# Attention steps placed between projection and gate passes of a conditioned hybrid decoder layer

## The chip, the cores and the metric

The kernel runs on one core of a Trainium2 chip. A core has a matrix engine (TensorE, PE in the profile, PEld for its weight loads), VectorE (DVE), ScalarE (ACT), GpSimd (POOL) and SyncE (SP), whose queue issues all DMA transfers here. Each engine runs its own instructions in program order; between engines only semaphores order the work. The metric is the device time of one execution in microseconds, the median of several runs.

## The reference, cut to what matters

One decoder layer for two request groups with shared weights: a prompt of 512 tokens and 8 samples of 4 new tokens each, 544 token columns in all, width 1024.

```python
def decoder_layer(x, c, lw, rel_bias, past):
    mod = (jax.nn.silu(c) @ lw['w_ada'] + lw['b_ada']).reshape(B, N_SUB, 3, D_MODEL)
    h = x + 0.5 * mod[:, 0, 2][:, None] * swiglu(modulate(x, gn[0], ...), lw['w_ffn1_gu'], lw['w_ffn1_down'])
    mix, state = token_mixer(modulate(h, gn[1], ...), lw, rel_bias, past)
    h = h + mod[:, 1, 2][:, None] * mix
    h = h + 0.5 * mod[:, 2, 2][:, None] * swiglu(modulate(h, gn[2], ...), lw['w_ffn2_gu'], lw['w_ffn2_down'])

def token_mixer(u, lw, rel_bias, past):
    q, kv_c, kv_s, kv_w, g_nsa, h_cv, b_cv, c_cv, g_merge = split_projection(u, lw['w_in'])
    o_nsa = ...   # compressed + selected + window attention, each branch with its own gate
    y_cv, conv_new = short_conv(h_cv, b_cv, c_cv, lw['w_conv'], conv_buf)
    merged = g_merge[:, :, 0] * (o_nsa @ lw['w_nsa_out']) + g_merge[:, :, 1] * (y_cv @ lw['w_conv_out'])
    return merged @ lw['w_out'], (kv_c, kv_s, win_new, conv_new)
```

`split_projection` applies a sigmoid to the 24 attention gates `g_nsa` and to the 2 x 1024 merge gates `g_merge`. The prompt has 8 blocks of 64 keys, so a selection of 16 takes them all; a sample has 17 and drops one of them by the compressed scores, and reads its past keys and values through a page table.

## The kernel before

Activations are held transposed, features on the partitions, 544 token columns in the free direction. Every product is made of three fp32r products: weights and activations are each split into a high half (ScalarE copies it, `split`, `wh`) and a low half (VectorE subtracts, `lo`, `wl`), and TensorE adds high times high, high times low and low times high. The work is cut into numbered *units*: one unit is one 128-column block of a weight matrix, loaded by SP into one of 4 `raw` buffers, split into one of 2 `wh`/`wl` buffers, and used by 48 matmuls of 272 columns (8 tiles of 128 rows), or 24 for matrices of 512 rows. I call the matmuls of one unit a *pass*. A unit's result fills two PSUM banks (`out2(slot)`), from which VectorE or ScalarE takes it.

The stages in time order: conditioning and compression of the cached keys; norm 0 and feed-forward 1; norm 1; 23 units of the input projection (`U_WIN`: queries, keys and values, attention gates, then four groups of three for the short convolution); 8 pairs of a merge gate unit and a convolution output unit (`U_MGB`); 8 units of the other merge gates (`U_MGA`), with the transposes of the values among them; compression of the prompt's keys (L1522); attention; then the output projection of attention (`U_NSA`), `U_OUT`, norm 2 and feed-forward 2. Nothing plans the order: it is the order in which each engine's code is written.

Attention has 24 prompt *jobs* (query block, branch, half of the heads). In each, TensorE makes four scores (L1603), VectorE adds the bias and takes the maximum (`p_add`, L1231), ScalarE takes the exponential (L815), VectorE scales (`p_scale`, L1251), TensorE transposes (L1615), ScalarE copies (`pTp`, L845), and TensorE multiplies by the values (L1628). The samples are done in two half batches of ten steps each, one step behind each job from the third on (`sample_step`): step 0 scores the new keys, 1 to 3 the cached ones, 4 sums the compressed probabilities and chooses the block that is dropped, 5 scales, 6 and 7 transpose, 8 multiplies by the values, 9 transposes the result.

Between a norm and its first unit VectorE and ScalarE produce the operand tiles one after the other (`u_lo`), and the first unit takes each as it comes (`ready`).

## Time and profile before

| | us |
|---|---|
| median of 3 runs (1538.55 to 1539.65) | 1538.82 |
| the profiled execution | 1537.42 |
| its span, first to last instruction | 1535.6 |
| TensorE busy in it | 1438.0 |
| VectorE, ScalarE, GpSimd busy | 555.3, 464.1, 112.9 |

The profile comes from one execution. [...] A wait is put down to the instruction whose semaphore came last. Instructions overlap by some tenths of a microsecond, so that the distance between two starts says more than a duration. Stages: norm 1 ends with the first matmul of the input projection at 591.05, the merge gates end at 862.50, and the output projection of attention starts at 1025.96.

### The profile page before, as it was taken

To read this page: it belongs to the slowest core of one execution; us is meant where nothing else is said; L and a number is where in the kernel's file an instruction comes from. 1 tells how busy PE (TensorE), PEld (TensorE's weight loads), DVE (VectorE), ACT (ScalarE), POOL (GpSimd) and SP (SyncE) were. 2 spreads that over 40 slices of the span, in tenths; PEclk is the share of its full clock that TensorE was granted. 3 is DMA by queue.
4 is the path that set the end of the run, shared out by engine and by line. 5 is a ranking of instruction groups with operands and counts; after the bars stand their busy time and mean duration, and the time that the engine had idled before them with its cause. 6 is when DMAs were issued, how large, how long until landed. Compare 5 with 4: busy or idle time off the path is not lost.

```text
span 1535.6 us, 28068 instructions
## 1 busy us (share of the span) xinstructions
PE 1438.0 (94%) x11334; PEld 1324.6 (86%) x11334; DVE 555.3 (36%) x1151; ACT 464.1 (30%) x751; POOL 112.9 (7%) x122
## 2 busy tenths in 40 slices
PE   7997999999999996999998989889789999999996
PEld 5676999999999996999998835459789999999995
DVE  0106323332323225335323274745443233232324
ACT  0115333332311114122212346643253333332111
POOL 0402000000001112000000000004320000000110
PEclk9998999999999997999999869989889999999998
DMA  9893444444433232232284323313212322323321
GB/s 347 291 369 110 139 162 137 163 137 161 133 92 87 84 103 54 86 93 69 83 97 157 126 81 102 99 50 116 83 56 82 95 83 86 92 65 87 86 84 67
DMA packets 83541, 180.21 MB, mean 117 GB/s; under 512 B 18341, under 2 KB 43429, under 8 KB 81742
## 3 DMA queue, kind: packets, MB, share of 16 engines
q1 hardware_dynamic: 83470, 179.23, 37.6%
q8 instruction: 49, 0.80, 0.2%
q14 instruction: 22, 0.18, 0.0%
HBM read 173.07 MB, written 10.28 MB: 119 GB/s over the span
## 4 chain that ended last, share of the span: by engine, by line
PE 86%; ACT 4%; DVE 4%; DMA 2%; SPq 2%; issue 2%; ACTq 0%; DVEq 0%
PE PS L1411 71%; PE PS L1334 4%; PE PS L1432 2%; DMA raw<-in_w_in 2%; PE PS L1603 1%; PE PS L1615 1%; SPq L574 1%; DVE rinv L937 1%; PE PS L1438 1%; PE PS L1315 1%; ACT uh L704 1%; PE PS L1348 1%; SPq L562 1%; PE PS L1628 1%; ACT sp L815 1%
## 5 line engine op out<-in xcount | busy, mean ns | idle before, releaser
L1411 PE MATMUL PS<-uh,wh 128*128 128x272 f32 x2032 | 428.8, 292 | 34.9 <-DVE ul L955 26.9
L930 DVE TENSOR_TENSOR wl<-raw,wh 128x1024 fp32r<-128x1024 f32 (+2 forms) x215 | 239.8, 1116 | 587.4 <-ACT wh L679 587.1
L679 ACT ACTIVATE wh<-raw 128x1024 fp32r<-128x1024 f32 (+2 forms) x215 | 203.6, 948 | 816.6 <-PE PS L1411 803.1
L1411 PE MATMUL PS<-uh,wl 128*128 128x272 f32 x2032 | 422.3, 290 | 0.0
L1411 PE MATMUL PS<-ul,wh 128*128 128x272 f32 x2032 | 421.7, 289 | 0.0
L1411 PEld LDWEIGHTS PS<-uh,wh 128*128 128x128 f32 x2032 | 320.5, 190 | 38.9 <-issue 36.1
L1411 PEld LDWEIGHTS PS<-ul,wh 128*128 128x128 f32 x2032 | 321.8, 190 | 0.0
L1411 PEld LDWEIGHTS PS<-uh,wl 128*128 128x128 f32 x2032 | 320.2, 190 | 0.0
L1411 PE MATMUL PS<-hh,wh 128*128 128x272 f32 x704 | 145.7, 288 | 0.9 <-DVE tmp L1004 0.9
L1411 PE MATMUL PS<-hh,wl 128*128 128x272 f32 x704 | 145.7, 288 | 0.0
L1411 PE MATMUL PS<-hl,wh 128*128 128x272 f32 x704 | 145.1, 288 | 0.0
L1411 PEld LDWEIGHTS PS<-hh,wh 128*128 128x128 f32 x704 | 110.7, 188 | 1.1 <-DVE tmp L1004 1.1
L1411 PEld LDWEIGHTS PS<-hl,wh 128*128 128x128 f32 x704 | 110.6, 188 | 0.0
L1411 PEld LDWEIGHTS PS<-hh,wl 128*128 128x128 f32 x704 | 109.9, 189 | 0.0
L1004 DVE TENSOR_TENSOR tmp<-sg,PS 128x544 f32<-128x544 f32 x44 | 31.8, 722 | 181.1 <-PE PS L1411 181.1
L615 POOL TENSOR_TENSOR sq<-h 128x544 f32 x28 | 30.6, 1093 | 857.3 <-DVE h L973 801.9
L1334 PE MATMUL PS<-ch,w 128*128 128x256 f32 x256 | 57.7, 387 | 0.7 <-DVE Fsb L891 0.7
L1334 PEld LDWEIGHTS PS<-ch,w 128*128 128x128 f32 x256 | 49.5, 195 | 8.6 <-issue 1.7
L1615 PEld LDWEIGHTS PS<-cst,sp 128*128 128x128 f32 (+4 forms) x192 | 23.5, 149 | 33.1 <-issue 24.2
L1615 PE MATMUL PS<-cst,sp 128*128 128x128 f32 (+4 forms) x192 | 38.9, 326 | 7.9 <-DVE sp L1251 7.8
L815 ACT ACTIVATE sp<-sp,stp 128x128 f32<-128x128 f32 (+7 forms) x96 | 44.5, 466 | 3.4 <-DVE stp L1235 3.3
L845 ACT ACTIVATE pTp<-PS 128x512 f32<-128x512 f32 (+4 forms) x48 | 28.1, 590 | 44.7 <-PE PS L1615 44.5
(221 smaller groups left out, 1244.5 us busy)
## 6 DMA issues: line engine op xcount, KB each, us to landing
raw<-in_w_gu SPq DMA_DIRECT2D x88, 512.0 KB, 3.6
ada_t<-in_w_ada_t SPq DMA_DIRECT2D x44, 512.0 KB, 4.4
raw<-in_w_in SPq DMA_DIRECT2D x39, 512.0 KB, 3.6
ada<-in_w_ada SPq DMA_DIRECT2D x7, 2048.0 KB, 9.7
raw<-in_w_dn SPq DMA_DIRECT2D x32, 384.0 KB, 3.1
raw<-in_w_dn SPq DMA_DIRECT2D x32, 320.0 KB, 2.9
ch<-in_cmp_pages SPq DMA_DIRECT2D x64, 128.0 KB, 4.1
kv<-in_sel_pages SPq DMA_DIRECT2D x128, 64.0 KB, 1.9
```

The lines of the kernel that those rows point to most:

```text
L562: e.dma_start(kv[:, b, 4 * part + j, :], d["sel_pages"][v][bass.ds(r, 1)].rearrange("o p n -> (o p) n")).then_inc(kv_in[1 + part], 16)
L574: e.dma_start(gs[32 * b:32 * b + 32, hb, br:br + 1], bass.AP(tensor=d["gscr"].tensor, offset=br * NH * TS + SQ * (4 * hb + b), ap=[[TS, NH ...
L615: e.tensor_tensor(sq[:, :], h[:, bass.ds(k, 1), :].rearrange("p o t -> p (o t)"), h[:, bass.ds(k, 1), :].rearrange("p o t -> p (o t)"), AL ...
L679: e.activation(wh[:, u % SPLITS, 0:n, :], raw[:, u % RAWS, 0:n, :], ACT.Copy).then_inc(hi_ready, 1)
L815: e.activation(sp[j % 3][:, r, 0:n], sp[j % 3][:, r, 0:n], ACT.Exp, bias=stp[:, j % 3, 0, r:r + 1], accum_out=stp[:, j % 3, 1, r:r + 1]).t ...
L845: e.activation(pTp[0:n, tr % 2, :], PS[0:n, 4 + tr % 2, :], ACT.Copy).then_inc(p_trc, 1)
L930: e.tensor_tensor(wl[:, u % SPLITS, 0:n, :], raw[:, u % RAWS, 0:n, :], f(wh[:, u % SPLITS, 0:n, :]), ALU.subtract).then_inc(lo_ready, 1)
L1004: e.tensor_tensor(halves(tmp[:, fi % 2, :]), halves(sg[:, fi % 2, :]), out2(2 * (fi % 2) + 1), ALU.mult).then_inc(psum_free, 2)
L1334: ins = mm(PS[:, 2 * (t % 2) + c, 1 - m:257 - m].rearrange("p (g j n) -> p g j n", g=2, n=8), w1[:, c, 8 * m + lp, :], ch[:, t % 2, :, lp, ...
L1411: ins = mm(o[:, a, :], w[:, u % SPLITS, k, :], x[:, k0 + k, HT * a:HT * a + HT], start=(first and k == 0 and w is wh and x is xh), stop=(l ...
L1432: ins = mm(PS[32 * q:32 * q + 32, ada_bank(fi), 0:P], csil[:, k, :], ada_t[:, n % 2, k, :], start=(k < 4), stop=(k >= 4), skip_group_check ...
L1615: ins = e.transpose(PS[0:n, 4 + tr % 2, P * s:P * s + P], sp[j % 3][:, s, P * kt:P * kt + n], ident)
```

## The change

- The 8 convolution output units (`U_CO`) follow the 23 of the input projection directly, and VectorE only copies their result (`mB`). All 16 merge gate units (`U_MG`) come behind them and share one pair of PSUM banks (`GATE_SLOT`).
- The gate units are cut into pieces of one operand tile, 6 matmuls (`fill`). Two whole units stand at the start of the prompt's attention, the other 112 pieces between scores, transposes and value products of the 24 jobs. ScalarE takes each gate out as a tanh of half the input, and splits the next weights behind it (`gate`). The sigmoid is rebuilt as tanh plus one, with the factor one half in `mods`; GpSimd multiplies and adds the convolution half (16 operations).
- The sample steps stand behind projection units (`SAMPLE_AT`): the first half batch behind blocks 10 to 19, the second behind blocks 20 to 22 and the first five convolution output units, its last two steps behind the first two gate units. The unit with the attention gates is moved forward to block 4, the transposes and the compression of the prompt's keys go behind blocks 9 to 14. PSUM slots in the projections are 3 instead of 4, score banks 3 instead of 4.
- SP issues page copies, biases, gate scalars and outputs between the weight loads of those units.
- Behind each norm the first two units run together, tile by tile (`two_units`).
- At the end of the first down projection and of `U_OUT`, VectorE's last `lo` stands behind the last residual.
- The two convolution states are packed by GpSimd into `conv_st` and sent in two transfers.

```diff
+WIN_BLOCK = [0, 1, 2, 3, 10, 4, 5, 6, 7, 8, 9] + list(range(11, 23))
...
+        SAMPLE_AT = {10 + k: (0, k) for k in range(10)}
+        SAMPLE_AT.update({20 + k: (1, k) for k in range(8)})
...
+                elif n == 5:
+                    attention_bias()
+                elif n == 6:
+                    cached_window(0, 0)
+                elif n in (7, 8):
+                    cached_pages(0, 0, n - 7)
...
+                load(U_CO + m, d["w_co"][m])
+                if m == 1:
+                    e.wait_ge(v_used, 1)
+                    cached_window(1, 0)
+                elif m in (2, 3):
+                    cached_pages(1, 0, m - 2)
...
+                elif m == 6:
+                    e.wait_ge(s_work, S_ITEMS + 4)
+                    cached_window(1, 1)
+                elif m == 7:
+                    cached_pages(1, 1, 0)
+            for x in range(2 * KD):
+                load(U_MG + x, d["w_in"][23 + x])
+                if x == 0:
+                    cached_pages(1, 1, 1)
+                elif x == 2:
+                    e.wait_ge(unit_used, U_MG)
+                    for g in range(2):
+                        e.dma_start(toep_g[g][:, :, :], d["toep"][:, GQ * g:GQ * g + GQ, :]).then_inc(toepg_in, 16)
...
                     for m in range(KD):
+                        e.wait_ge(gate_free, m + 1)
+                        e.wait_ge(psum_free, O_CO + m + 1)
+                        e.tensor_tensor(sgB[:, m % 2, :], sgB[:, m % 2, :], mB(m), ALU.mult).then_inc(gated, 1)
+                        e.wait_ge(gated, m + 1)
+                        e.tensor_tensor(mB(m), mB(m), sgB[:, m % 2, :], ALU.add).then_inc(mb_ready, 1)
+                    e.wait_ge(mb_ready, KD)
+                    for m in range(KD):
                         e.wait_ge(psum_free, O_NSA + m + 1)
-                        e.tensor_tensor(work(m), work(m), mB[:, m, :], ALU.add).then_inc(m_ready, 1)
...
+            def gate(x):
+
+                e.wait_ge(unit_used, U_MG + x + 1)
+                if x < KD:
+                    if x >= 2:
+                        e.wait_ge(mb_ready, x - 1)
+                    dst = sgB[:, x % 2, :]
+                else:
+                    dst = sgA[:, x - KD, :]
+                e.activation(halves(dst), out2(GATE_SLOT), ACT.Tanh, scale=0.5).then_inc(gate_free, 1)
+                split(U_MG + x + 2)
...
                 for m in range(KD - 2, KD):
-                    for j in range(4):
+                    for j in range(3 if m == KD - 1 else 4):
                         if ud + 4 * m + j + 2 < U_END:
                             lo(ud + 4 * m + j + 2)
                     e.wait_ge(unit_used, ud + 4 * m + 4)
                     residual(m, 0, gate, m % 2, od, n)
+                if ud + 4 * KD + 1 < U_END:
+                    lo(ud + 4 * KD + 1)
...
+                if n in SAMPLE_AT:
+                    s_step(*SAMPLE_AT[n])
+            for m in range(KD):
+                lo(U_CO + m + 2)
+                e.wait_ge(unit_used, U_CO + m + 1)
+                if m == 0:
+                    e.wait_ge(kv_out, 6 * 16)
+                    e.wait_ge(conv_packed, 2)
+                e.tensor_copy(halves(mB(m)), out2((23 + m) % 3)).then_inc(psum_free, 1)
+                if 23 + m in SAMPLE_AT:
+                    s_step(*SAMPLE_AT[23 + m])
...
             p_add(0)
-            sample_queries()
+            lo(U_MG + 2)
+            s_output(1)
+            lo(U_MG + 3)
...
+                for at_ in fills(j - 1) if j else ():
+                    if (j - 1, at_) in GATE_DONE:
+                        lo(U_MG + GATE_DONE[j - 1, at_] + 2)
             lo(U_NSA + 1)
...
             for m in range(KD):
-                lo(U_OUT + m + 2)
+                if m < KD - 1:
+                    lo(U_OUT + m + 2)
                 e.wait_ge(unit_used, U_OUT + m + 1)
                 residual(m, 0, 24 + 16, m % 4, O_OUT, KD)
+            lo(U_OUT + KD + 1)
...
+            def two_units(u, slot, xh, xl, ready):
+
+                e.wait_ge(lo_ready, u + 2)
+                for k in range(KD):
+                    e.wait_ge(ready[0], ready[1] + k + 1)
+                    for v in range(2):
+                        o = out2(slot + v)
+                        for w, x in ((wh, xh), (wh, xl), (wl, xh)):
+                            for a in range(2):
+                                ins = mm(o[:, a, :], w[:, (u + v) % SPLITS, k, :], x[:, k, HT * a:HT * a + HT],
+                                         start=(k == 0 and w is wh and x is xh), stop=(k == KD - 1 and w is wl))
+                        if k == KD - 1:
+                            ins.then_inc(unit_used, 1)
+
...
+                def first_tile():
+
+                    e.wait_ge(psum_free, og)
+                    two_units(ug, 0, uh, ul, (u_lo, 8 * nn))
+                    if first:
+                        late_partial(0, 0)
+                        e.wait_ge(part_copied, NADA + 1)
+                        late_partial(1, 0)
+                        e.wait_ge(ada_copied, NADA)
+                        late_total(0, 0)
...
-            for n in range(23):
-                if n >= 4:
-                    e.wait_ge(psum_free, O_WIN + n - 3)
-                unit(U_WIN + n, n % 4, uh2, ul2, 0, True, True, 0, (u_lo, 8) if n == 0 else None)
-            for m in range(KD):
-                e.wait_ge(psum_free, O_MGB - 1 + m if m < 2 else O_MGB + 2 * m - 2)
-                unit(U_MGB + 2 * m, 2 * (m % 2), uh2, ul2, 0, True, True)
-                unit(U_MGB + 2 * m + 1, 2 * (m % 2) + 1, yh, yl, 0, True, True, 0, (y_lo, 0) if m == 0 else None)
-
...
+            two_units(U_WIN, 0, uh2, ul2, (u_lo, 8))
+            for n in range(2, 23):
+                if n >= 3:
+                    e.wait_ge(psum_free, O_WIN + n - 2)
+                unit(U_WIN + n, n % 3, uh2, ul2, 0, True, True)
+                if n == 9:
+                    prep_values(0)
+                elif n == 11:
+                    prep_values(1)
+                elif n == 12:
+                    prep_compress()
+                elif n == 13:
+                    prep_keys()
+                elif n == 14:
+                    prep_tails()
+                if n in SAMPLE_AT:
+                    s_step(*SAMPLE_AT[n])
+            for m in range(KD):
...
+            chunk = [0]
+
+            def fill(n):
+
+                for _ in range(n):
+                    x, k = divmod(chunk[0], KD)
+                    chunk[0] += 1
+                    if k == 0:
+                        e.wait_ge(lo_ready, U_MG + x + 1)
+                        if x:
+                            e.wait_ge(gate_free, x)
+                        else:
...
+
+            def p_score(j, s):
                 i, br, _ = JOBS[j]
...
-            p_score(0)
-            p_score(1)
+            e.wait_ge(psum_free, O_CO + KD)
+            for s in range(3):
+                p_score(0, s)
+            fill(KD)
+            s_step(1, 8)
+            p_score(0, 3)
+            for s in range(3):
+                p_score(1, s)
+            fill(KD)
+            s_step(1, 9)
+            p_score(1, 3)
...
-                    p_score(j + 2)
-                if sample_step(j):
-                    s_step(*sample_step(j))
-                for tr in range(TR0[j], TR0[j + 1]):
-                    p_turn(j, tr)
+                more = j + 2 < len(JOBS)
+                if more:
+                    p_score(j + 2, 0)
+                    p_score(j + 2, 1)
+                fill(1)
+                if more:
+                    p_score(j + 2, 2)
+                fill(1)
+                for t in range(turns(j)):
+                    p_turn(j, TR0[j] + t)
+                    if t == 0 and more:
+                        p_score(j + 2, 3)
+                    fill(1)
                     if late:
                         p_value(*late)
-                    late = (j, tr)
+                    late = (j, TR0[j] + t)
+                if "end" in fills(j):
+                    fill(1)
             p_value(*late)
 
 
+            e.wait_ge(gate_free, 2 * KD)
```

Two places in the order of instructions. The first is on ScalarE, at the last convolution blocks of the input projection. Before (`wh` is a split, `yh` the high half of the convolution result):

```order
L679 ACTIVATE wh<-raw 128x1024 x3
L761 ACTIVATE yh<-tmp 128x544
L679 ACTIVATE wh<-raw 128x1024 x2
L679 ACTIVATE wh<-raw 128x512
L761 ACTIVATE yh<-tmp 128x544
L679 ACTIVATE wh<-raw 128x1024
```

After, from the end of block 16's transposes (`pT` are copies of transposed sample probabilities, `sx` is the sample result on its way to the last transpose, `oh` its high half, `ss` a sample exponential):

```order
L825 ACTIVATE pT<-PS 63x128
L744 ACTIVATE wh<-raw 128x1024 x2
L869 ACTIVATE yh<-tmp 128x544
L836 ACTIVATE sx<-PS 128x128
L840 ACTIVATE oh<-PS 64x4x4 x8
L744 ACTIVATE wh<-raw 128x1024
L831 ACTIVATE ss,st<-ss,st 128x63
L744 ACTIVATE wh<-raw 128x512
L831 ACTIVATE ss,st<-ss,st 128x544
```

Sample copies now stand behind `yh`, which itself waits for VectorE's convolution; before, only splits stood there.

The second is on TensorE, in the first job with 512 keys. Before (`kT,qT` scores, `cst,sp` transposes, `pTp` value products, `cst,ss` transposes of the samples):

```order
L1603 MATMUL PS<-kT,qT 128x512 x4
L1615 MATMUL PS<-cst,sp 31x128 x4
L1628 MATMUL PS<-pTp,vcp 64x256 x2
L1603 MATMUL PS<-kT,qT 128x512 x4
L1571 MATMUL PS<-cst,ss 128x128 x8
L1615 MATMUL PS<-cst,sp 128x128 x4
L1628 MATMUL PS<-pTp,vcp 64x256 x2
L1615 MATMUL PS<-cst,sp 128x128 x4
L1628 MATMUL PS<-pTp,vn 64x256 x2
L1615 MATMUL PS<-cst,sp 128x128 x4
```

After (`uh`, `ul` with `wh`, `wl` are the gate pieces of L1746):

```order
L1760 MATMUL PS<-kT,qT 128x512 x2
L1746 MATMUL PS<-uh,wh 128x272 x2
L1746 MATMUL PS<-ul,wh 128x272 x2
L1746 MATMUL PS<-uh,wl 128x272 x2
L1760 MATMUL PS<-kT,qT 128x512
L1746 MATMUL PS<-uh,wh 128x272 x2
L1746 MATMUL PS<-ul,wh 128x272 x2
L1746 MATMUL PS<-uh,wl 128x272 x2
L1772 MATMUL PS<-cst,sp 128x128 x4
L1760 MATMUL PS<-kT,qT 128x512
L1746 MATMUL PS<-uh,wh 128x272 x2
L1746 MATMUL PS<-ul,wh 128x272 x2
```

The four scores of a job are pulled apart, and six gate matmuls stand between each pair of steps.

## Rows read from the trace of the kernel before

**Rows 1.** The page, section 1 and the clock by slice of 38.4 us.

```profile
PE 1438.0 (94%) x11334; PEld 1324.6 (86%) x11334; DVE 555.3 (36%) x1151; ACT 464.1 (30%) x751; POOL 112.9 (7%) x122
...
PEclk9998999999999997999999869989889999999998
```

**Rows 2.** Windows: length, busy time (count) of each engine, clock, DMA share, GB/s.

```profile
598.90:862.50 263.60, 255.87 (x2042) 255.42 (x2043) 89.11 (x126) 56.74 (x70) 0.00 (x0) 0.99 0.38 97
862.50:1025.96 163.46, 138.06 (x974) 76.62 (x972) 98.46 (x479) 89.46 (x291) 0.00 (x0) 0.83 0.31 90
873.00:889.50 16.50, 14.34 (x81) 8.36 (x80) 11.41 (x82) 10.39 (x46) 0.00 (x0) 0.50 0.51 157
812.07:815.49 3.42, 3.42 (x20) 3.42 (x20) 1.26 (x2) 0.00 (x0) 0.00 (x0) 0.64 0.72 188
590.00:600.00 10.00, 8.71 (x44) 8.03 (x45) 8.76 (x13) 8.59 (x14) 7.55 (x13) 0.70 0.00 1
```

**Rows 3.** Timeline of TensorE, attention stage: start, duration, instruction, idle before and releaser.

```profile
907.33 4.39 PE L1603 MATMUL PS<-kT,qT 64*128 64x512 f32 x8 [3.99 <-DVE stp L1231]
...
928.60 1.99 PE L1603 MATMUL PS<-kT,qT 64*128 64x512 f32 x8
```

**Rows 4.** Timeline of ScalarE, projections: two splits that wait for passes.

```profile
606.76 1.06 ACT L679 ACTIVATE wh<-raw 128x1024 fp32r<-128x1024 f32 x1 [4.91 <-PE PS L1411]
...
612.74 1.06 ACT L679 ACTIVATE wh<-raw 128x1024 fp32r<-128x1024 f32 x1 [4.91 <-PE PS L1411]
```

**Rows 5.** Timeline of TensorE, attention stage, single operations.

```profile
862.50 7.25 PE L1522 MATMUL PS<-chp,w1p 128*128 128x64 f32 x64
...
892.16 1.06 PE L1557 MATMUL PS<-kv,qb 128*32 128x512 f32 x8
...
939.04 2.83 PE L1586 MATMUL PS<-kv,pT 128*32 128x128 f32 x96
...
949.38 0.65 PE L1628 MATMUL PS<-pTp,vn 128*64 128x256 f32 x4
...
949.96 0.66 PE L1615 MATMUL PS<-cst,sp 128*128 128x128 f32 x4
```

**Rows 6.** Timeline of TensorE, first pass behind the second norm.

```profile
591.05 0.79 PE L1411 MATMUL PS<-uh,wh 128*128 128x272 f32 x2 [9.02 <-DVE ul L955]
591.64 0.66 PE L1411 MATMUL PS<-ul,wh 128*128 128x272 f32 x2
592.09 0.66 PE L1411 MATMUL PS<-uh,wl 128*128 128x272 f32 x2
```

**Rows 7.** Timeline of VectorE, end of the first down projection.

```profile
576.76 1.23 DVE L930 TENSOR_TENSOR wl<-raw,wh 128x1024 fp32r<-128x1024 f32 x1 [2.53 <-ACT wh L679]
...
577.90 0.50 DVE L965 SCALAR_TENSOR_TENSOR h<-PS,mods,h 128x272 f32<-128x272 f32 x1
...
582.13 0.72 DVE L935 TENSOR_SCALAR rinv<-PS 128x544 f32<-128x544 f32 x1 [3.03 <-PE PS L1424]
```

**Rows 8.** Timeline of ScalarE, a convolution block of the projections.

```profile
678.44 1.06 ACT L679 ACTIVATE wh<-raw 128x1024 fp32r<-128x1024 f32 x1 [4.92 <-PE PS L1411]
...
684.00 0.66 ACT L761 ACTIVATE yh<-tmp 128x544 fp32r<-128x544 f32 x1 [4.50 <-DVE tmp L1094]
```

**Rows 9.** Timeline of VectorE, sample steps 4 and 5.

```profile
902.35 0.22 DVE L1181 COPY sx<-PS 128x63 f32<-128x63 f32 x1 [1.62 <-PE PS L1563]
...
912.95 0.76 DVE L1208 TENSOR_SCALAR ss<-ss,st 128x1056 f32<-128x1056 f32 x1
```

**Rows 10.** Timeline of TensorE, first gate pass after late weights.

```profile
811.71 0.79 PE L1411 MATMUL PS<-uh,wh 128*128 128x272 f32 x2 [7.73 <-DVE wl L930]
```

**Rows 11.** Timeline of the SP queue, page copies.

```profile
874.13 19.55 SPq L562 DMA_DIRECT2D kv<-in_sel_pages  x32
```

**Rows 12.** Timeline of GpSimd and VectorE, output projection of attention.

```profile
1051.81 1.78 POOL L637 TENSOR_TENSOR sg<-sg,mB 128x544 f32<-128x544 f32 x1 [2.00 <-DVE sg L1286]
...
1052.86 1.82 DVE L930 TENSOR_TENSOR wl<-raw,wh 128x1024 fp32r<-128x1024 f32 x1 [0.49 <-ACT wh L679]
```

More of the change, by code:

```diff
@@ L405, in nkeys, with turns, fills @@
             return 8 * i + 7 if br == 0 else P * (i + 1)
+        def turns(j):
+            return TR0[j + 1] - TR0[j]
+        def fills(j):
+            return ["pair", "third"] + [("turn", t) for t in range(turns(j))] + (["end"] if turns(j) <= 2 else [])
+        GATE_DONE = {}
+        step_ = 2 * KD
+        for j_ in range(len(JOBS)):
+            for at_ in fills(j_):
+                step_ += 1
+                if step_ % KD == 0:
+                    GATE_DONE[j_, at_] = step_ // KD - 1
         def toep_cols(i, br):
@@ L851, in _ @@
-                if k in (0, 1, 4):
-                    s_exps(hb, {0: 0, 1: 1, 4: 2}[k])
-                if k == 9:
-                    s_output(hb)
-            split(U_NSA)
-            split(U_NSA + 1)
+                gate_at(j, "pair")
+                gate_at(j, "third")
+                for t in range(turns(j)):
+                    p_turned(j, t)
+                    if turns(j) > 1 and more and t < 2:
+                        p_exp_head(j + 1, 2 * t)
+                        p_exp_head(j + 1, 2 * t + 1)
+                    gate_at(j, ("turn", t))
+                    if t == 0 and j and closes(j - 1):
+                        p_output(j - 1)
@@ L857, in _ @@
+                gate_at(j, "end")
             p_output(len(JOBS) - 1)
```

649 lines of the change are left out of this document (336 added, 313 removed).

## The prediction

> **What bounds the kernel now.** I read the page first: TensorE is busy for 94% of the span, and the slices in which its clock is below full lie at the start, at slice 16 and from slice 23 to 30 [rows 1]. So only two things can be won: time in which TensorE waits, and time in which it works at half clock. Next the windows over the two stages that the change touches. The projections (598.90 to 862.50) run at clock 0.99 with TensorE busy for 255.87 of 263.60 us; the attention stage (862.50 to 1025.96) takes 163.46 us, at clock 0.83, with 138.06 busy, and much of that at half clock [rows 2]. The timeline says why: TensorE stands 3.99 us for VectorE's bias-and-maximum pass, and the 512-key scores behind it take 4.39 us where the same eight records take 1.99 later [rows 3]. The stage is a chain through VectorE and ScalarE with TensorE dragged along; the change puts TensorE work that waits for nobody into it.
>
> **What TensorE must do, at full clock.** One pass over 1024 rows of weights (48 matmuls) has a pitch of 5.98 us, the distance of two ScalarE splits that each wait for one, 0.1245 us a matmul; a four-tile pass costs half, 2.99 [rows 4]. From the full-clock part of the attention stage: four transposes and two value matmuls alternate 0.585 us apart, 48 of each, 56.2 us; the scores of one job cost 1.99 us (512 keys) and by their widths about 1.5, 1.1 and 0.6 (384, 256, 128), four jobs each, and eight compressed jobs by estimate what 128 keys cost: 26 us; a half batch of samples costs 3 x 1.03 for cached keys, 2.4 for 15 transposes at the prompt's pace, 3.75 for values (2.83 of them over cached pages) and some 1.5 for three small steps, so 21.5 us for two; the preparation 7.25 for the compression, and by my estimate 2.6 for its second layer and the transposes of values and gates [rows 3, 5]. Attention in all: 113.5 us of TensorE in a stage of 163.46. So 50 us stand open.
>
> **The change, part by part.**
>
> *Two passes by operand.* Now each of the eight operand tiles of a norm serves one pass, then two. The first matmul comes at 591.05, after 9.02 us of idling, and the first pass runs at half clock: its matmul pairs stand 0.45 us apart, against 0.25 at full clock, and TensorE hardly waits for tiles [rows 6]. The two passes end at 606.7 before (the ScalarE split that waits for the second starts at 606.76 [rows 4]). The 10 us from 590 have clock 0.70 [rows 2], 6 us at half, so 4.9 from the first matmul on. After: these hold 21 of the 96 matmuls, the other 75 need 9.4, end 605.3. But the third pass needs its weights split, which can start only when the last tile of the first pass is through: 0.96 + 1.14 us behind 604.6, so TensorE stands until 606.8. Gain nil, at each of three norms; bounds -2 to +2 together. I take 0.
>
> *Low half after the residual.* At the end of the down projection VectorE first waits for the split and computes `wl` (576.76, 1.23 us) and only then the residual (577.90), on which the norm hangs [rows 7]. Moved behind, the residual starts at about 575.7: 2.2 us earlier. The moved 1.14 us lies in the 3.03 us in which VectorE waits for the norm sum. It happens twice (the second at the output projection): 4.4 us.
>
> *Sample steps behind the projection passes.* Each step is hidden by a pass of 5.97 us only if VectorE and ScalarE answer within it. They run what is queued ahead first: the split, `wl`, the evacuation and, every third block, the convolution. That chain is in the trace already: the split starts 678.44, `yh` ends 684.66, 6.2 us after the pass ended [rows 8]. Behind it now stand sample copies for which TensorE waits:
> - block 16: the transposes need the scaled probabilities. From the end of block 14: split 1.0, `wl` 1.14, evacuation 0.66, block choice 4.3 (from 902.35 to 906.66), exponential 2.6 with its table load, then split, `wl`, evacuations 1.5 and the scaling 2.0: 15.4, against 12.9 of TensorE work: 2.5 us. Then the second group waits for a ScalarE copy queued behind the block's `yh`: 6.2 + 0.6 less what has passed, but started late with VectorE: 5.0. One more of 1.1.
> - block 19: the last transpose waits for the `sx` copy, behind `yh`: 6.2 + 0.27 = 6.4 us.
> - first convolution pass: it wants the last `yl`, which a gate pass used to cover; 6.9 us less 1.0 of scores and three tiles at 0.75: 2.8.
> - the second half in the 2.99 us passes: block choice to scaling take 11.4, TensorE has 6.25: 5.2, and 1.4 in the copies behind.
> - start of the gate passes: last evacuation 2.9, `sx` copy 1.9, and the score that waits for an evacuation behind the output split 3.3.
> Sum 32.5 us of new waits. The start of the block choice and the end of the scaling are in [rows 9]; the exponential is taken as 1.3 us, a width of 1056 at ScalarE's pace for `wh`, and a table load of another 1.3.
>
> *Prompt attention between gate passes.* Each of the 24 jobs now holds 4 to 6 pieces of six matmuls (0.75 us). Over the stage TensorE has 82 + 94 us. VectorE had 98.46 us in the whole stage before and ScalarE 89.46 [rows 2]; they lose some 20 and 10 of samples and gain 16 x 1.15 and 16 x 1.5: about 97 and 104. TensorE becomes the bound. I leave 3.4 us for the seven places where a gate pass waits for its bank and 1.9 at the end: 5.3. [...] Most seams follow no open wait, so I take 0.03, 3 us; bounds 0 and 16.
>
> *Transfers.* The 7.73 us for late weights at 811.71 [rows 10] go, since the output DMAs no longer stand ahead of them. In their place page copies stand ahead of weight loads on the SP queue: 32 take 19.55 us, so 16 take 9.8 [rows 11], and the 24 gate scalars go at a similar pace each. A full pass is 5.97 us and the four raw tiles keep SP ahead, so those cost nothing; from the second convolution pass to the first gate pass SP has about 45 us to issue and TensorE about 53 to pass. Cost 0, upper bound 10.
>
> *GpSimd adds.* Sixteen new operations of 1.78 us lie beside VectorE. Beside such an add VectorE's `wl` took 1.82 us [rows 12] instead of the 1.23 elsewhere [rows 7]. Price 0 to 9.6 us (16 x 0.6); covered by the pass that is a whole pass ahead, so 0. [...]
>
> *Clock.* After 7.73 us of idling TensorE ran 20 matmuls in a stretch of 3.42 us that holds 27 at full clock; after 9.02 us it kept half clock for those 4.9 us more, 2.4 us lost [rows 2, 6]. The four waits of 5 us and more (5.0, 6.4, 5.2 and 1.9 + 3.3) I price at 2.0 each, 8 us; bounds 0 and 34 (17 us of half clock behind each, as in the low stretch from 873 to 889 [rows 2]). [...]
>
> **The sum.** Clock time at which the attention output projection starts: 606.8, plus 1968 matmuls x 0.1245 = 245.0, plus 113.5, plus waits 32.5 + 5.3, plus 3 and 8: 1014.1; before it was 1026.0. Gain 11.9, and 4.4 from the residuals: 16.3 us. Against the profiled execution (1537.4, its span 1535.6 and 1.8 around it) 1521; the median of the runs lies 1.4 higher: 1522.5. I say 1523.
>
> **Rivals.**
> - *Waits that shrink* (A): TensorE keeps full clock through waits of 5 us and the seams cost nothing: 11 us less, 1512. For it: the 3.99 us wait was followed by half clock [rows 3], so against; but the surroundings there were small matmuls, here dense passes.
> - *Late weights* (B): SP's issue slots run over among the short passes, or contended page copies land late, so that TensorE waits 10 us: 1533. For it: 45 of 53 us filled; against: elsewhere the queue is ahead.
> - *VectorE beside GpSimd* (C): the 9.6 us come onto the path: 1533.
> - *Half clock through the sample steps* (D), the slow side: each of the four long waits brings 17 us at half clock instead of about 4, 34 us lost instead of 8, 1549. It decides from 24 us lost, 6 a wait. For it: the stretch at 873; against: there fine-grained work ran on between waits, and the projection after 811.71 lost only 7 matmuls, some 1 us, in its next 3.42 [rows 2].
>
> **Chances.** Forecast 50%, A 20%, B 12%, C 8%, D 10%. Faster by over 0.2% (3 us, about what a measurement here can tell from none): 0.88; within: 0.03, from B and C together; slower: 0.09. Range 1509 to 1536.
>
> **What would show it.** Right: the attention stage proper, from the last convolution pass to the output projection, at clock 0.98 or more, with no wait over 2 us behind its first two gate passes; waits of about 5 to 6.4 us for ScalarE's `pT` and `sx`; `wl` behind the residual at both places. Wrong: TensorE waiting for `raw` loads; `PEclk` under 0.9 in the projections; gate passes waiting for VectorE.

## The result, and the profile after

| | before | after |
|---|---|---|
| median of 4 runs each | 1538.68 | 1554.18 |
| range | 1537.54 to 1539.65 | 1553.40 to 1555.59 |
| ratio to before, 95% interval | | 1.0102 (1.0085 to 1.0120) |
| span of the profiled execution | 1535.6 | 1552.7 |

The change makes the kernel 15.5 us slower. I had forecast 1523, 31 us less than it takes. The page of after, section 1 and the clock by slice of 38.8 us, against [rows 1]:

```profile
PE 1451.5 (93%) x11334; PEld 1331.7 (86%) x11334; DVE 562.4 (36%) x1152; ACT 466.3 (30%) x752; POOL 138.4 (9%) x140
...
PEclk9998999999999998999988999999989999999998
```

The clock is what I had hoped for. (It is the granted clock of TensorE as a share of full; half clock is a stretch at 0.50, as 591.05 to 595.90 in the kernel before, where the pairs of [rows 6] stand 0.45 us apart.) But the same 11334 matmul instructions keep TensorE busy 13.5 us longer. Three windows of after follow (length, busy time and count of PE, PEld, DVE, ACT and POOL, clock, DMA share, GB/s). The first runs from the third pass of the projections to the last convolution output pass, the second holds the first two gate units, and the third is the woven stage, from 847.00 to the output projection of attention at 1047.16, where before had 1025.96 [rows 2]:

```profile
606.37:815.40 209.03, 185.51 (x1501) 175.26 (x1501) 89.49 (x186) 45.74 (x74) 0.42 (x2) 0.94 0.42 131
815.40:847.00 31.60, 23.30 (x235) 21.34 (x234) 8.32 (x44) 7.66 (x30) 5.37 (x4) 0.84 0.43 151
847.00:1047.16 200.16, 194.57 (x1220) 136.90 (x1221) 94.68 (x374) 93.21 (x256) 19.75 (x12) 0.99 0.10 29
```

In the woven stage the clock is 0.99 and TensorE is busy for 97% of the time, and yet it takes some 30 us more than its parts in my forecast. So hardly anything is waited for; the matmuls themselves are dearer. The waits of TensorE over all three windows, the eight largest sums (waiting line and releaser: us in total, times, longest):

```profile
PE PS L1664 <- ACT sx L836: 8.3, 2, 6.5
PE PS L1644 <- ACT pT L822: 8.0, 4, 5.1
PE PS L1644 <- DVE ss L1215: 6.3, 2, 5.3
PE PS L1760 <- DVE stp L1320: 3.3, 1, 3.3
PE PS L1760 <- DVE mB_last L1305: 3.1, 1, 3.1
PE PS L1503 <- DVE yl L1271: 2.7, 1, 2.7
PE PS L1503 <- issue: 2.0, 1, 2.0
PE PS L1746 <- ACT sgA L886: 2.0, 4, 0.9
```

These are the waits that I forecast, within 0.5 us in sum. What I missed stands in the timeline of TensorE in the woven stage (start, duration, instruction, idle before). First the start of a gate piece, then one score matmul alone (`x2`, since each shows as two records) with the next piece behind it; then a value product, four transposes, a piece and the next value product; then two score matmuls (`x4`):

```profile
899.92 0.52 PE L1746 MATMUL PS<-uh,wh 128*128 128x272 f32 x2
...
900.87 1.12 PE L1760 MATMUL PS<-kT,qT 64*128 64x512 f32 x2
901.92 0.52 PE L1746 MATMUL PS<-uh,wh 128*128 128x272 f32 x2
902.27 0.41 PE L1746 MATMUL PS<-ul,wh 128*128 128x272 f32 x2
902.53 0.41 PE L1746 MATMUL PS<-uh,wl 128*128 128x272 f32 x2
...
907.23 0.65 PE L1788 MATMUL PS<-pTp,vn 128*64 128x256 f32 x4
907.82 0.66 PE L1772 MATMUL PS<-cst,sp 128*128 128x128 f32 x4
908.23 0.50 PE L1746 MATMUL PS<-uh,wh 128*128 128x272 f32 x2
908.56 0.41 PE L1746 MATMUL PS<-ul,wh 128*128 128x272 f32 x2
908.81 0.42 PE L1746 MATMUL PS<-uh,wl 128*128 128x272 f32 x2
909.15 0.65 PE L1788 MATMUL PS<-pTp,vn 128*64 128x256 f32 x4
...
911.66 1.13 PE L1760 MATMUL PS<-kT,qT 64*128 64x512 f32 x4
912.72 0.52 PE L1746 MATMUL PS<-uh,wh 128*128 128x272 f32 x2
```

Read the distances between starts. One score matmul of 512 keys holds TensorE from 900.87 to 901.92, 1.05 us. Two of them hold it from 911.66 to 912.72, 1.06 us. Before, four of them took 1.92 [rows 3]: they start at 928.60, and the next matmul starts at 930.52. And a gate piece of six matmuls takes 0.95 us between two places of scores (899.92 to 900.87) and 0.92 behind transposes (908.23 to 909.15), where six matmuls of a whole pass take 0.75 [rows 4]. The transposes ahead of such a piece gain by it: 0.41 (907.82 to 908.23) where they took 0.58 ahead of a value product.

The ledger, by distances between starts summed over all rows of a kind, from the third pass (606.37) to the output projection of attention (1047.16), in us:

| | forecast | measured |
|---|---|---|
| 96 score matmuls | 25.6 | 44.4 |
| 16 gate units | 95.6 | 118.1, of which 3.4 half clock |
| other passes | 149.4 | 158.6, of which 5.2 half clock |
| transposes of the prompt | 28.1 | 23.2 |
| value products of the prompt | 28.1 | 28.1 |
| samples and preparation | 31.4 | 31.0 |
| waits | 37.8 | 37.4 |
| allowances: seams 3, half clock 8 | 11.0 | in the rows above |
| sum | 407.0 | 440.8 |

The 25.6 are the sum of the prediction's own prices, which it rounds to 26; so its sum over this stretch is 407.3. A seam is a change from one kind of matmul to another; the 3 us are for the 112 that the gate pieces bring. "Half clock" is what a row took beyond its full-clock price; by the granted clock the sample, score and transpose rows lost some 4 us more to it, 1.3 of them in the scores.

Outside this stretch the kernel did 0.4 us better than forecast: the two residuals gave 3.3 us each instead of 2.2, and some more behind them, but the profiled execution came 2.75 us late to its first feed-forward pass (132.50 against 129.75). It was 1.06 late at the sum of the first norm already (116.72 against 115.66), and 3.4 us at half clock followed, which the execution before did not have. That is scatter: in the kernels below this pass starts anywhere from 129.6 to 133.4, and the same conditioning stage stands ahead of it.

### The profile page after: what moved, and what is told of

Read it like the earlier page. It is cut to its first block, busy times and chain, and to the rows that moved or that the text cites. A ratio compares the mean times of both kernels' runs of the same rounds, so it can differ in the third digit from the quotient of the medians.

```text
span 1552.7 us, 28107 instructions
## 1 busy us (share of the span) xinstructions
PE 1451.5 (93%) x11334; PEld 1331.7 (86%) x11334; DVE 562.4 (36%) x1152; ACT 466.3 (30%) x752; POOL 138.4 (9%) x140
## 4 chain that ended last, share of the span: by engine, by line
PE 92%; DVE 4%; ACT 2%; issue 1%; DMA 1%; SPq 0%; DVEq 0%; ACTq 0%
PE PS L1503 64%; PE PS L1746 7%; PE PS L1426 4%; PE PS L1760 3%; PE PS L1517 3%; PE PS L1788 2%; PE PS L1538 2%; PE PS L1772 2%; DVE rinv L1015 1%; PE PS L1544 1%; PE PS L1407 1%; PE PS L1440 1%; ACT wh L744 1%; PE PS L1476 0%; DMA vec<-in_vec 0%
## 5 line engine op out<-in xcount | busy, mean ns | idle before, releaser
L1503 PE MATMUL PS<-uh,wh 128*128 128x272 f32 x1680 | 353.6, 292 | 3.5 <-DVE wl L1008 3.5
L1503 PE MATMUL PS<-uh,wl 128*128 128x272 f32 x1680 | 348.2, 289 | 0.0
L1503 PE MATMUL PS<-ul,wh 128*128 128x272 f32 x1680 | 347.9, 289 | 0.0
L1503 PEld LDWEIGHTS PS<-uh,wh 128*128 128x128 f32 x1680 | 264.6, 189 | 7.7 <-issue 5.6
L1503 PEld LDWEIGHTS PS<-ul,wh 128*128 128x128 f32 x1680 | 265.1, 189 | 0.0
L1503 PEld LDWEIGHTS PS<-uh,wl 128*128 128x128 f32 x1680 | 263.9, 190 | 0.0
L667 POOL TENSOR_TENSOR sq<-h 128x544 f32 x28 | 30.6, 1093 | 858.2 <-DVE h L1051 802.5
L1746 PE MATMUL PS<-uh,wh 128*128 128x272 f32 x256 | 65.2, 337 | 3.6 <-ACT sgA L886 2.0
L1746 PEld LDWEIGHTS PS<-uh,wh 128*128 128x128 f32 x256 | 39.6, 194 | 32.0 <-issue 30.4
L1320 DVE CUSTOM_DVE_ANT_0 sp<-PS,toep_g 128x128 f32<-128x128 f32 (+7 forms) x96 | 34.4, 385 | 56.6 <-PE PS L1760 52.0
L1746 PE MATMUL PS<-ul,wh 128*128 128x272 f32 x256 | 54.1, 293 | 0.0
```

Source lines behind the costliest of these rows:

```text
L1320: e.tensor_tensor_reduce(sp[j % 3][:, s, 0:n], PS[:, (GQ * j + s) % 3, 0:n], toep_g[g][:, r, toep_cols(i, br)], 1.0, -3e38, ALU.add, ALU.m ...
L1503: ins = mm(o[:, a, :], w[:, u % SPLITS, k, :], x[:, k0 + k, HT * a:HT * a + HT], start=(first and k == 0 and w is wh and x is xh), stop=(l ...
L1746: ins = mm(o[:, a, :], w[:, (U_MG + x) % SPLITS, k, :], u[:, k, HT * a:HT * a + HT], start=(k == 0 and w is wh and u is uh2), stop=(k == K ...
```

## The experiments

The theory that the runs are to test starts from what the trace of the changed kernel shows. It prints passes and transposes of whole blocks with 128 rows and 128 columns (`128*128`), score matmuls with 64 rows (`64*128`), value products with 64 columns (`128*64`). By the kernel (`head`, `p_score`), scores 0 and 2 of a job read partitions 0 to 63, scores 1 and 3 partitions 64 to 127. One score of 512 keys took 1.05 us, and scores 0 and 1 together 1.06 (911.66 to 912.72), their records starting 0.007 us apart: two in different halves ran side by side. The theory: cutting the four scores of a job into two, one and one leaves two without a partner, and each change of shape costs a seam, as a gate piece of 0.92 to 0.95 us instead of 0.75 does above. Rivals: a seam of fixed size and nothing else; VectorE's and ScalarE's chain as the bound; and, for the sample steps, waits that only move. The kernel before was timed again with every group of runs: its medians were 1540.4 (beside `pairs`, `rows_0213`, `act_first`, `group4`), 1541.5 (beside `pairs_same`, `late_half`, `one_by_one`, `lo_late`) and 1541.6 (beside the other four). The changed kernel was not. So a gain over it ("less" below) is a difference of medians from different groups. By the ratios to the kernel before it would be up to some 4 us larger, so a smaller difference than that shows in the traces at most. The stretch of the ledger, from the third pass to the output projection of attention, took 440.8 us in the changed kernel and is given for the others.

**pairs.** Edit of the changed kernel:

```
                 fill(1)
-                if more:
-                    p_score(j + 2, 2)
                 fill(1)
 ...
                     if t == 0 and more:
+                        p_score(j + 2, 2)
                         p_score(j + 2, 3)
```

> The changed kernel (1554), with the third score matmul of each prompt job issued beside the fourth, behind the first transposes, instead of alone between two gate pieces; TensorE's order alone changes. Row-half theory: a score matmul uses 64 of the 128 rows, heads 0 and 1 lie in different halves and run side by side, so two adjacent scores of 512 keys cost 1.06 us and one alone costs 1.05. The change makes three slots of two; this kernel makes them two again: less 1.05 + 0.84 + 0.63 + 0.41 us for four jobs of each width (11.7) and about 0.33 for six of the compressed ones (2), and 22 pairs of gate pieces become one, 0.17 each (3.7): 17 us less, 1537. Seam theory (each change between kinds of matmul costs a fixed amount, whatever stands beside it): only the merged pieces count, about 4 us less, 1550. Chain theory (VectorE and ScalarE set the stage's pace): nothing, 1554.

Measured: 1539.2 (1538.06 to 1540.98), ratio to before 0.9996 (0.9981 to 1.0010). In the ledger scores fall from 44.4 to 33.8 and gate units from 118.1 to 113.5; the stretch takes 426.7. The seam theory alone (1550) and the chain theory (1554) are out, and this one edit, expected at 1537, gives back the whole loss.

**rows_0213.** Edit of the kernel before, in `p_score` and `p_add`:

```
-                for s in range(GQ):
+                for x, s in enumerate((0, 2, 1, 3)):
```

(`x` takes the place of `s` in the two counts that are waited for.)

> The kernel before (1538.7), its four scores of a job issued and evacuated in the order 0, 2, 1, 3, everything else as it was. Heads 0 and 2 use one half of TensorE's rows, 1 and 3 the other. Row-half theory: only 2 and 1 still run side by side, so a job takes three slots instead of two: its eight records of 512 keys at full clock take about 3.1 us instead of 1.99, and all scores some 14 us more; how much of it reaches the end depends on the waits around, between 0 and 14, say 7: 1546. Seam theory: the order within a job is of no account, 1.99 us and 1538.7.

Measured: 1548.4 (1542.3 to 1550.6), ratio 1.0063 (1.0042 to 1.0085). A job of 512 keys in it, with the row of [rows 3] as its counterpart:

```profile
930.84 1.99 PE L1603 MATMUL PS<-kT,qT 64*128 64x512 f32 x8
```

1.99 us, not 3.1, and all its scores only 1.5 us more (37.4 against 35.9). The theory as I had put it missed: four scores in a row took 1.92 us from start to start in both orders. The single records of this job start at 0, 0.013, 0.533, 0.546, 0.962, 0.975 us and so on, two by two, as they do in the kernel before. The time did rise by 8 us, of which its profiled execution shows 5 (2.8 before the first pass, 1.4 in the wait of [rows 10], 1.5 in scores, less 0.9 behind attention). It is the fastest of the six, and the cause of the other 3 to 8 us stays open.

**pairs_same.** As `pairs`, with heads 0 and 2 as the first pair and 1 and 3 as the second (`head(j, (0, 2, 1, 3)[s])`, and VectorE in that order).

> The kernel of the run named pairs (1539), where now heads 0 and 2 make up the first pair of score matmuls and heads 1 and 3 the second, so both of a pair lie in the same half of TensorE's rows; all counts and places stay. Row-half theory: the two of a pair can't run side by side, a pair of 512 keys takes 1.05 + 0.85 = 1.9 us instead of 1.06, and over all 0.85 + 0.64 + 0.43 + 0.21 us for eight pairs of each width: 17 us more, 1555. Rival (any adjacent score matmuls overlap, whichever rows they use, as the order 0, 2, 1, 3 of four in a row cost nothing in the run named rows_0213): 1539 and 1.06 us.

Measured: 1555.8 (1555.0 to 1557.2), ratio 1.0090 (1.0066 to 1.0114), 16.5 more than `pairs` by the medians and 14.5 by the ratios. The stretch takes 441.5, 14.8 more: scores 50.1 instead of 33.8, waits 1.7 less, every other row within 0.2. TensorE in it, then in `pairs`, at the first jobs of 512 keys:

```profile
887.62 1.98 PE L1760 MATMUL PS<-kT,qT 64*128 64x512 f32 x4
889.53 0.52 PE L1746 MATMUL PS<-uh,wh 128*128 128x272 f32 x2
```

```profile
883.91 1.13 PE L1760 MATMUL PS<-kT,qT 64*128 64x512 f32 x4
...
884.97 0.51 PE L1746 MATMUL PS<-uh,wh 128*128 128x272 f32 x2
```

1.91 us from start to start against 1.06, with the same count at the same place in the order. The single records of `pairs` start at 0, 0.007, 0.534 and 0.540 us, two by two, those of this run at 0, 0.534, 0.963 and 1.392, one by one. So a pair between gate pieces overlapped where its two lie in different halves (1.06), and not where they lie in the same (1.91); four in a row, two of each half, overlapped in both orders (1.92 in `rows_0213` and before). How TensorE pairs them up no row shows, nor what it does at a seam; measured is only its length, a gate piece of up to 0.95 us beside another shape instead of 0.75.

**group4.** The pieces of the changed kernel saved up and issued four at a time, at every fourth place.

> The changed kernel (1554), its gate pieces saved up and issued four at a time (24 matmuls) at every fourth place, attention's order untouched: 28 seams in each direction instead of 112. Seam and row-half theories: the pieces' excess over 0.1245 us a matmul falls from some 19 us to 5, the transposes lose 4 to 6 of what they gain by standing ahead of a piece, and most scores stand beside each other again (some 8 less): 16 us less, 1538, if TensorE stays the bound. Cover theory (a piece at each place is needed, because VectorE and ScalarE answer within one piece but not at once): new waits of 0.5 to 1 us at most of the 80 uncovered places eat that up, 1554 or more.

Measured: 1559.9 (1559.6 to 1564.4), ratio 1.0136 (1.0108 to 1.0164). The cover theory has the time right, though its waits have another form. Seams go nearly as expected: gate units take 114.5 us with 12.7 of half clock in them, so 101.8 at full clock against 114.7 in the changed kernel. Scores take 3.2 less, not 8. But waits rise by 9 us and half clock by 10, and transposes lose 5. The new waits are not short ones at most places, but eight of 0.8 to 2.2 us, all of one kind, in an execution 4.5 us above the median (L1768 is the score matmul, moved eight lines by the edit):

```profile
860.77 0.55 PE L1768 MATMUL PS<-kT,qT 64*128 64x128 f32 x2 [2.19 <-DVE stp L1320]
...
876.80 0.40 PE L1768 MATMUL PS<-kcp,qT 64*128 64x31 f32 x2 [2.18 <-DVE stp L1320]
...
1016.90 0.70 PE L1768 MATMUL PS<-kT,qT 64*128 64x256 f32 x2 [1.66 <-DVE stp L1320]
```

The fourth score of a job waits for VectorE to free one of the three banks. So here the fine pieces were worth their seams, and the place of the scores was not.

**pairs_after_value.** As `pairs`, with the second pair behind `p_value` instead of before the gate piece.

> The kernel of the run named pairs (1539), its second pair of scores moved one piece later, behind the value matmuls instead of between the first transposes and the gate piece. Transposes and gate pieces both use all 128 rows and columns and stand side by side without a seam (0.41 us for four transposes ahead of a piece, 0.58 ahead of values or scores); scores and values use half. Seam theory as the runs have left it (only a change of the array's shape costs): one seam of 0.17 us less in each of 22 jobs, 3.7 us less, 1535. Rival: VectorE gets these scores about 1.5 us later and TensorE comes to wait for it at the next pair: 1539 or more.

Measured: 1536.5 (1535.7 to 1537.7), ratio 0.9968 (0.9956 to 0.9981), 2.7 less than `pairs` (423.8 for the stretch, 2.8 less). Transposes take 20.3 (from 22.8): that is the seam's part, 2.4 where 3.7 was expected. Scores take 31.1 (from 33.8), and this is no seam. In `pairs` nine of 43 pairs took 3.9 us more in all than a pair of their width does; here three do, by 0.2. In the one where the trace names a releaser, the fourth score waits for VectorE to free its bank (`pairs`):

```profile
893.83 1.12 PE L1760 MATMUL PS<-kT,qT 64*128 64x512 f32 x2
896.04 1.12 PE L1760 MATMUL PS<-kT,qT 64*128 64x512 f32 x2 [1.09 <-DVE stp L1320]
```

Gate units and value products give back 1.6, for the most part half clock, and waits 0.4. The rival's 1539 did not come.

**act_first.** ScalarE's `s_step` of the changed kernel ahead of its `yh` copy.

> The changed kernel (1554), with ScalarE's sample step ahead of the convolution's yh copy in the blocks where both stand. If TensorE's 5.13 and 6.52 us waits (blocks 16 and 19) come from the queueing behind yh, both shrink to about 1 us, and some half clock behind them goes: 10 to 12 us less, 1543. Rival: yh then waits for TensorE's sample step, so VectorE's low half and its next evacuation come late and TensorE waits there instead: 1554.

Measured: 1542.3 (1538.6 to 1546.1), ratio 1.0025 (1.0008 to 1.0042), 12 less than the changed kernel (427.0 for the stretch, 13.8 less: 9.4 in waits, the rest mostly half clock in the passes). ScalarE in after, and then in this kernel, behind block 16:

```profile
716.49 0.66 ACT L869 ACTIVATE yh<-tmp 128x544 fp32r<-128x544 f32 x1 [4.50 <-DVE tmp L1269]
717.05 0.58 ACT L822 ACTIVATE pT<-PS 128x512 f32<-128x512 f32 x1
```

```profile
713.01 0.60 ACT L822 ACTIVATE pT<-PS 128x512 f32<-128x512 f32 x1 [0.59 <-PE PS L1644]
714.36 0.60 ACT L822 ACTIVATE pT<-PS 128x512 f32<-128x512 f32 x1 [0.75 <-PE PS L1644]
716.91 0.66 ACT L871 ACTIVATE yh<-tmp 128x544 fp32r<-128x544 f32 x1 [1.96 <-DVE tmp L1269]
```

ScalarE had stood 4.50 us for `yh`, with the copy that TensorE waits for behind it. Now that idle time takes the copies, `yh` comes no later (this kernel is 0.42 us behind at block 16), and TensorE's waits of 5.13 and 6.52 are 0.69 and 1.37.

**late_half.** `SAMPLE_AT` with steps 6 and 7 of the second half batch at 28 and 30 instead of 26 and 27.

> The changed kernel (1554), with steps 6 and 7 of the second half batch of samples behind the sixth and eighth convolution pass instead of the fourth and fifth. Step 6 waited 5.28 us for VectorE's scaled probabilities behind a block choice of 11.4 us; with two more passes of 2.99 us in between that wait is covered, and the copies behind it (0.75 and 0.83) stay or go; 2 us of half clock behind the wait go too: 6 to 8 us less, 1547. Rival (the step's chain runs on into the next wait, at the first gate pass, where the last evacuation is already 3.10 us late): the gain is below 3 us, since steps 6 and 7 now stand right ahead of that pass and ScalarE's and VectorE's work for them with it: 1552.

Measured: 1553.5 (1553.1 to 1555.1), ratio 1.0073 (1.0050 to 1.0097), 0.7 less (439.5 for the stretch, 1.3 less). The rival was right. The wait of 5.28 is gone and the 3.10 of the first gate pass is 0.90, but these came:

```profile
795.61 0.50 PE L1504 MATMUL PS<-yh,wh 128*128 128x272 f32 x2 [2.81 <-DVE wl L1009]
...
804.83 0.66 PE L1645 MATMUL PS<-cst,ss 128*128 128x128 f32 x4 [0.96 <-ACT pT L823]
...
815.32 0.50 PE L1645 MATMUL PS<-cst,ss 128*32 128x128 f32 x3 [3.37 <-ACT pT L823]
```

VectorE's block choice now delays a low half instead of the step itself.

**start.** Three moves around the first two gate units: the first of them ahead of the first three scores; ScalarE's `sx` copy ahead of the second tanh; VectorE's `s_output(1)` behind `p_add(1)`.

> The changed kernel (1554) with the three waits around its first two gate passes taken away: the first gate pass ahead of the first three scores (they waited 3.10 us for the last evacuation), ScalarE's sx copy ahead of the second tanh (1.83 us), VectorE's sample output behind its next bias-and-maximum pass (3.33 us). Wait theory: the three go, 8 us less, and with them up to 5 us of half clock behind them (820 to 823 and 844 to 850): 1543. Rival: VectorE's chain is what is late here, and the waits only come together in one later on: 1550 or more.

Measured: 1547.7 (1546.3 to 1548.5), ratio 1.0042 (1.0030 to 1.0054), 6.5 less (434.2 for the stretch, 6.6 less). Two waits went (3.10 and 1.83); the third stayed, so that my reason for it was wrong:

```profile
835.79 0.27 PE L1765 MATMUL PS<-kcp,qT 64*128 64x7 f32 x1 [3.18 <-DVE stp L1324]
```

**one_by_one.** `two_units` as two calls of `unit`, only the first with `ready`.

> The changed kernel (1554), with the two passes behind each norm run one after the other again, only the first of them waiting for operand tiles. My prediction gave the two passes by operand nothing: the third pass then waits for its weights. If that holds, 1554 within 2 us, and the wait of 1.7 to 1.8 us for the third pass's weights vanishes while the first pass ends later. Rival (two passes per tile keep TensorE denser at the start, so half clock ends earlier: pairs at half clock cover 3.8 us here, 5.2 before): up to 3 times 1 us lost, 1557.

Measured: 1553.6 (1551.1 to 1555.3), ratio 1.0070 (1.0051 to 1.0089), beside 1.0102 for the changed kernel, from another group of runs. From the second norm to the first wait of the samples it takes 120.9 us (591.62 to 712.50) against 121.5 (590.43 to 711.90). So the part is worth nothing, or loses some 0.5 us a place.

**lo_late.** The last `lo` behind the last residual, in the kernel before.

> The kernel before (1538.7) with one part of the change alone: at the end of the first down projection and of the output projection VectorE computes the last low half behind the residual. Prediction's term: 2.2 us at each place, 1534.3. The trace of the changed kernel shows more: from the last projection pass to the first FFN or input pass 15.07 us became 11.76, since the sum's matmuls also keep full clock (1.18 instead of 2.18 us): 3.3 each, 1532. Rival (the gain comes from the two passes by operand standing with it): 0, 1538.7.

Measured: 1535.8 (1530.0 to 1537.5), ratio 0.9956 (0.9940 to 0.9972), 5.7 to 6.8 less. VectorE in it:

```profile
575.82 0.50 DVE L965 SCALAR_TENSOR_TENSOR h<-PS,mods,h 128x272 f32<-128x272 f32 x1 [1.39 <-PE PS L1415]
...
577.05 1.23 DVE L930 TENSOR_TENSOR wl<-raw,wh 128x1024 fp32r<-128x1024 f32 x1
...
578.98 0.72 DVE L935 TENSOR_SCALAR rinv<-PS 128x544 f32<-128x544 f32 x1 [0.71 <-PE PS L1428]
```

The wait of 3.03 [rows 7] is 0.71. The sum's matmuls, which took 2.18 us at half clock behind a wait of 3.35, take 1.19 behind one of 1.06: that is the third microsecond at this place, which the prediction did not count.

**best1 and best2.** The changed kernel with `pairs`, `act_first` and `start`; and with `pairs_after_value`, `act_first`, `start` and `late_half`.

> The changed kernel with three of the edits together: score matmuls in pairs (15 us less by itself), ScalarE's sample step ahead of the yh copy (12 less), and the start edits of the run named start (8 to 11 less if they work). They touch different stretches, so they should add up: 1554 - 15 - 12 - 10 = 1517, against 1540 for the kernel before. If they share a limit (VectorE's chain in the woven stage), 1525 or more.

> As best1, with the second pair behind the value matmuls (3.7 us less if the seam theory holds) and steps 6 and 7 of the second half batch two passes later (2 less, measured as 1554 to 1553.5 alone; with the gate pass now ahead of the first scores its late copies have more cover). Adding up: 1517 - 3.7 - 2 = 1511. If either edit only moves its wait, 1517.

Measured: best1 1524.4 (1521.1 to 1526.3), ratio 0.9885 (0.9866 to 0.9904); best2 1518.0 (1514.6 to 1519.3), ratio 0.9843 (0.9823 to 0.9863). best2 is 24 us faster than before by its ratio, and its median is 36 below the changed kernel's. Both came out 7 us above what was expected, in part because `start` gives 6.5 and not the 10 that I put in. The edits nearly add up. Singly the medians give 17.7, 11.9, 6.5 and 0.7, together 36.8 against 36.2; for best1 it is 33.4 against 29.8. In the stretch the sums are 38.7 against 34.8 and 34.5 against 29.0, so 4 to 5 us are lost in combination, and I don't know where. The page of best2:

```profile
PE 1429.9 (94%) x11334; PEld 1323.3 (87%) x11334; DVE 562.9 (37%) x1152; ACT 466.0 (31%) x752; POOL 138.9 (9%) x140
...
PEclk9998999999999998999989999999999999999998
```

From its third pass to the output projection of attention it takes 406.0 us, against 440.8 for the changed kernel and 419.5 before (606.50 to 1025.96). That is less than my forecast for the changed kernel, 407.0, by other means: scores 30.6, waits 23.8.

## Why the prediction was wrong, point by point

- **The step that failed** is the price of TensorE's work in the woven stage: "the scores of one job cost 1.99 us (512 keys)", carried over into a stage where they no longer stand together, and the price of the 112 seams, one for each gate piece set between attention's matmuls: "I take 0.03, 3 us; bounds 0 and 16". Scores cost 18.8 us more than that (44.4 against 25.6). By my estimate nearly half of these are lost overlap, and the rest seams. Four scores of 512 keys in a row take 1.92, a pair 1.06 and one alone 1.05, so a further pair in a row adds some 0.86, and about 0.2 are paid once. Call the time of a pair, or of one alone, a slot: a job now needs three for its scores, where four in a row took two. By the estimate the third costs 0.86, 0.64, 0.43 and 0.21 by width, 8.6 for four jobs each; two more seams of 0.2 in each of 24 jobs are 9.6, and 1.3 is half clock. `pairs_same` agrees: it makes the two slots of `pairs` four, and scores rise by 16.3. Gate pieces cost 19.1 more at full clock (118.1 less 3.4, against 95.6), 0.17 for each of 112. The passes cut by sample steps cost 4.0 more. Transposes cost 4.9 less: ahead of a gate piece four take 0.41 us, ahead of a value product 0.58. Together 37.0, where I had allowed 3. The lost overlap had no term at all in the sum, and no bound.
- No run shows the 0.03 us a seam, 3 in all, that the sum uses, nor its lower bound of nothing; the runs showed 0.17 for each of the 112 pieces. The upper bound, 16, is 112 times 0.14, by which the first pair of [rows 6] took longer after a wait (0.59 against 0.45), and that is no seam. So the bound was wrong too, not only the value. The rows at hand gave sums only: transposes and value products 0.58 us apart in [rows 5], four scores in 1.99 in [rows 3]. The price of one alone, which I needed, stands in neither.
- **Waits**: 32.5 + 5.3 forecast, 37.4 measured, with their places and releasers. `act_first` shows that the reason given for the two largest, a copy behind `yh`, is the right one. That the sum is so close is partly luck. The first transposes of block 16 waited 1.06, not 2.5. And for the first convolution pass 6.9 less 1.0 less three times 0.75 is 3.65, not the 2.8 in the prediction; 2.70 was measured.
- **Half clock**: 8 forecast, 8.6 in passes and gate units, and some 4 in the other rows. The waits of 5 us and more cost some 1.7 each where a run took them away (`act_first`: two waits less, and the passes take 155.2 instead of 158.6), so rival D, 17 us at half clock behind each, did not come.
- **Transfers**: TensorE waits for no `raw` load in these stages, and the 7.73 us of [rows 10] are gone. Rival B is out.
- **GpSimd beside VectorE**: `wl` takes 1.54 us beside the adds, instead of the 1.22 elsewhere in this stage, at four places, and the add beside it takes 2.2 instead of 1.35. No matmul waits for it; 0 was right, rival C out.
- **Two passes by operand**: 0, as forecast (`one_by_one`).
- **Low half after the residual**: 6.7 by the trace of `lo_late` instead of 4.4. From the norm sum to the next pass it takes 12.27 and 11.73 us at the two places, before it was 15.63 and 15.07.
- **Rival A** (waits shrink) did not happen. None of my rivals had the cause: the fine mix of matmul shapes took 37.0 us more than the prices of its parts. The slow side had 9%, all on the clock.
- The signs I named as proof nearly all came (clock 0.99 in the woven stage, though 0.97 from the last convolution pass on where I had said 0.98; waits of 5.1 and 6.5 us for `pT` and `sx`), while the time went the other way. They tested waits and clock, not the length of the work.

## What to carry to other kernels

Before weaving matmuls of two shapes, price each alone, in a pair and in a row, by distances between starts: the sum over uncut blocks gave 25.6 us for scores that took 44.4 when cut. Here it paid to keep two scores of different row halves together (1.06 us, against 1.91 for two of one half and 1.05 for one alone), and to put transposes beside gate pieces (0.41 for four, against 0.58 beside value products) and scores beside value products (`pairs_after_value`, 2.7 us less); in another kernel measure these first. A TensorE that is 97% busy at clock 0.99 was still the loss; compare its total busy time for equal instruction counts (1451.5 against 1438.0 us for 11334).

## What the runs showed of the hardware that I had not expected

- Two fp32 score matmuls of 512 columns in different halves of the rows: 1.06 us; one alone 1.05; two in the same half 1.91; four in a row 1.92, in the order of halves A B A B as in A A B B. In the single records of a pair the two start 0.007 us apart.
- A change from full width to half cost about 0.17 us: four transposes take 0.41 ahead of a gate piece and 0.58 ahead of a value product. A gate piece takes 0.75 among its own, 0.86 behind a score and ahead of transposes, 0.93 behind transposes and ahead of a value product, and 0.95 between two places of scores (medians of the woven stage at full clock). It isn't the number format: transposes are plain fp32 and pieces fp32r, and in `pairs_after_value` four transposes between two pieces take 0.35.
- A single score of 512, 384, 256 or 128 keys takes 1.05, 0.84, 0.63 or 0.42 us: 0.21 for each 128 keys and 0.21 once.
- Equal code before the first feed-forward pass reached it 129.6 to 133.4 us into the span: up to 3.8 us of scatter between executions.
